# First tokens and weights in slices, ScalarE's table loaded first, normed tokens made before the small vectors

## What is computed

```
h  = rms_norm(x, norm_mix)                 # x * rsqrt(mean(x*x) + eps) * gain
p  = h @ w_in                              # columns: conv x | conv b | conv c | u | gate_a | gate_b
ya = W_conv_out( b * dwconv3_causal(c * x_conv) )
yb = GLU( gelu( Re(C s_t) + D u_t ) ),     s_t = A_bar s_{t-1} + B_bar u_t
x  = x + W_o( sigmoid(gate_a) * ya + sigmoid(gate_b) * yb )
x  = x + HierMoE( rms_norm(x) )            # 32 experts, 512 wide, top 1 group then top 2 experts
out = rms_norm(x)
```

## Time and profile before

| | us |
|---|---|
| median of three executions | 711.07 |
| lowest and highest | 710.84 and 711.48 |
| the profiled execution | 712.18 |
| its span, first to last instruction | 710.5 |
| PE busy in the span | 546.5 (77%) |
| PEld busy | 329.6 (46%) |
| DVE busy | 206.6 (29%) |
| ACT busy | 63.9 (9%) |
| POOL busy | 39.9 (6%) |

### The profile page before, as it was taken

How to read it: one execution, slowest core, us unless ns; L and a number is a source line. 1 busy time by engine, 2 the same in 40 slices (tenths; PEclk the granted TensorE clock), 3 DMA queues, 4 the chain that set the end, 5 groups by cost and what they waited for, 6 DMA issues and landing times.

```text
span 710.5 us, 7587 instructions
## 1 busy us (share of the span) xinstructions
PE 546.5 (77%) x3259; PEld 329.6 (46%) x3259; DVE 206.6 (29%) x443; ACT 63.9 (9%) x128; POOL 39.9 (6%) x68
## 2 busy tenths in 40 slices
PE   8999999999999999898583482594567348247765
PEld 7888888788878456363141140141114114012411
DVE  4888896969423043000000010000000001000002
ACT  3010000002011023000010000000000000000002
POOL 5001111111100011000000000000000000000000
PEclk9999999999999999999896797788779679778988
DMA  8960903274089657999999999999999999999993
GB/s 336 424 288 0 355 2 132 105 266 185 24 351 428 261 215 284 409 428 428 431 427 427 429 429 428 426 431 427 428 429 429 428 428 431 427 428 430 426 425 136
DMA packets 18901, 241.92 MB, mean 341 GB/s; under 512 B 2353, under 2 KB 2481, under 8 KB 4402
## 3 DMA queue, kind: packets, MB, share of 16 engines
q1 hardware_dynamic: 18432, 239.83, 81.1%
q10 hardware_dynamic: 434, 1.58, 0.5%
HBM read 240.35 MB, written 1.05 MB: 340 GB/s over the span
## 4 chain that ended last, share of the span: by engine, by line
PE 52%; DMA 43%; issue 1%; DVE 1%; SPq 1%; ACT 1%; DVEq 0%; POOL 0%; PEldq 0%; ACTq 0%
DMA x_region<-in_w_down 38%; PE bank L1138 28%; PE bank L1399 8%; DMA rot_region<-in_last_halves 4%; PE bank L1272 4%; PE bank L1150 2%; PE bank L1440 2%; PE bank L1127 2%; PE bank L1358 1%; PE bank L1461 1%; PE bank L1391 1%; SPq L474 1%; DMA ring<-in_mix 1%; PE bank L1242 1%; PE bank L1252 1%
## 5 line engine op out<-in xcount | busy, mean ns | idle before, releaser
L1391 PE MATMUL bank<-ring,z_region 128*32 128x512 f32 x672 | 113.2, 681 | 69.3 <-DMA ring<-in_w_up 68.8
L1138 PE MATMUL bank<-x_region,ring 128*128 128x256 f32 x640 | 141.0, 381 | 1.7 <-ACT ring L626 1.1
L1138 PEld LDWEIGHTS bank<-x_region,ring 128*128 128x128 f32 x640 | 120.8, 190 | 21.3 <-ACT ring L626 2.8
L1399 PE MATMUL bank<-ring,z_region 128*32 128x512 f32 x192 | 57.0, 760 | 49.9 <-DMA x_region<-in_w_down 49.9
L1391 PEld LDWEIGHTS bank<-ring,z_region 128*32 128x32 f32 x672 | 30.3, 123 | 113.8 <-issue 113.8
L1062 DVE TENSOR_TENSOR z_region<-z_region,bank 128x512 f32<-128x512 f32 x8 | 8.2, 1026 | 203.5 <-PE bank L1391 191.4
L1391 PE MATMUL bank<-rot_region,z_region 128*32 128x512 f32 x112 | 50.9, 609 | 12.1 <-DMA ring<-in_w_gate 10.5
L1399 PE MATMUL bank<-late_region,z_region 128*32 128x512 f32 x96 | 56.9, 760 | 0.0
L1399 PE MATMUL bank<-x_region,z_region 128*32 128x512 f32 x96 | 56.9, 760 | 0.0
L1399 PEld LDWEIGHTS bank<-ring,z_region 128*32 128x32 f32 x192 | 14.8, 136 | 87.3 <-issue 87.3
L1391 PE MATMUL bank<-s_region,z_region 128*32 128x512 f32 x112 | 51.1, 610 | 0.0
(11 more groups left out here) (245 smaller groups left out, 531.5 us busy)
## 6 DMA issues: line engine op xcount, KB each, us to landing
ring<-in_w_up SPq DMA_DIRECT2D x28, 2048.0 KB, 39.1
ring<-in_mix SPq DMA_DIRECT2D x16, 2048.0 KB, 10.6
ring<-in_w_gate SPq DMA_DIRECT2D x14, 2048.0 KB, 45.6
ring<-in_w_down SPq DMA_DIRECT2D x12, 2048.0 KB, 35.4
ring<-in_first SPq DMA_DIRECT2D x8, 2048.0 KB, 13.0
rot_region<-in_w_gate SPq DMA_DIRECT2D x7, 2048.0 KB, 36.2
s_region<-in_w_gate SPq DMA_DIRECT2D x7, 2048.0 KB, 40.7
late_region<-in_w_down SPq DMA_DIRECT2D x6, 2048.0 KB, 43.0
```

The lines of the kernel that those rows point to most:

```text
L1138: ins = MM(dst, w[:, k, n * P:(n + 1) * P], rhs[:, k, :], start=k == 0, stop=k == kn - 1)
L1391: ins = MM(bank[to][quarter(e), :], xT[:, k, quarter(e)], of_expert[e][:, FF * k:FF * k + FF], start=k == 0, stop=k == KD - 1)
L1399: ins = MM(bank[6 + h][quarter(e), :], actT[:, c, quarter(e)], of_expert[e][:, D * c + 512 * h:D * c + 512 * h + 512], start=c == 0, stop= ...
```

## The change

- `x_columns` is laid out as one array of eight slices and comes in five pieces: slice 0, slice 1, slices 2 and 3, slices 4 and 5, slices 6 and 7. Unit 0 comes in eight pieces, one for each slice k, each directly behind the piece of x that it is used with. All of it stays on SP's queue, behind the vectors and ahead of all else.
- ACT copies two constants as its first instruction, behind a small wait for POOL, so that its table load comes ahead of the wait for the vectors and x.
- DVE makes `hT` directly behind `zc`, ahead of the twenty operations on 16 columns.
- PE waits for each slice of unit 0; the sum of squares moves from behind k = 2 to behind k = 3, and the row of 1/rms from behind k = 4 to behind k = 5.

```
-            for c in range(U_PIECES):
-                sp.dma_start(x_raw[:, 2 * c:2 * c + 2, :].rearrange("p k t -> p (k t)"), x_columns[c]).then_inc(x_cols_in[c], 16)
-                if c == 0:
-                    first_piece(0)
-            for c in range(1, U_PIECES):
-                first_piece(c)
+            for (k0, k1), landed in zip(X_PIECES, x_cols_in):
+                sp.dma_start(x_raw[:, k0:k1, :].rearrange("p k t -> p (k t)"), x_columns[:, T * k0:T * k1]).then_inc(landed, 16)
+                for k in range(k0, k1):
+                    sp.dma_start(w8(U_U)[:, k, :], mix[U_U, :, 512 * k:512 * k + 512]).then_inc(u_in[k], 16)
...
-            nc.gpsimd.memset(halfneg[:], -0.5)
+            nc.gpsimd.memset(halfneg[:], -0.5).then_inc(halves_set, 1)
...
+            act.wait_ge(halves_set, 1)
+            nc.scalar.activation(stat[:, 0:2], halfneg[:], ACT.Copy)
+
             act.wait_ge(cols_in, 16)
             for k in range(KD):
-                if k % 2 == 0:
-                    act.wait_ge(x_cols_in[k // 2], 16)
+                for (k0, _), landed in zip(X_PIECES, x_cols_in):
+                    if k == k0:
+                        act.wait_ge(landed, 16)
...
-            for piece in range(U_PIECES):
-                dve.wait_ge(x_cols_in[piece], 16)
+            for piece in range(PAIRS):
+                if piece == 0:
+                    dve.wait_ge(x_cols_in[0], 16)
+                dve.wait_ge(x_cols_in[piece + 1], 16)
...
             ins.then_inc(zc_ready, 1)
+
+            dve.wait_ge(row_ready, 1)
+            dve.wait_ge(h_raw_ready, KD)
+            for piece in range(PAIRS):
+                V.tensor_tensor(hT[:, 2 * piece:2 * piece + 2, :], h_raw[:, 2 * piece:2 * piece + 2, :],
+                                rstd_row.unsqueeze(1).to_broadcast([P, 2, T]), ALU.mult).then_inc(hT_ready, 2)
...
-            dve.wait_ge(row_ready, 1)
-            dve.wait_ge(h_raw_ready, KD)
-            for piece in range(U_PIECES):
-                V.tensor_tensor(hT[:, 2 * piece:2 * piece + 2, :], h_raw[:, 2 * piece:2 * piece + 2, :],
-                                rstd_row.unsqueeze(1).to_broadcast([P, 2, T]), ALU.mult).then_inc(hT_ready, 2)
...
             for k in range(KD):
-                if k % 2 == 0:
-                    pe.wait_ge(u_in[k // 2], 16)
+                pe.wait_ge(u_in[k], 16)
                 pe.wait_ge(h_raw_ready, k + 1)
...
-                if k == 2:
-                    pe.wait_ge(square_step, 2 * U_PIECES - 1)
+                if k == 3:
+                    pe.wait_ge(square_step, 2 * PAIRS - 1)
...
-                if k == 4:
+                if k == 5:
                     pe.wait_ge(diag_ready, 1)
```

More of the change, by code:

```diff
@@ L31 @@
 MIX_UNITS = 17
-U_PIECES = 4
+X_PIECES = ((0, 1), (1, 2), (2, 4), (4, 6), (6, 8))
+PAIRS = KD // 2
 U_BANKS = (2, 3, 6, 7)
@@ L170, in block_kernel @@
         gate_b = ring[:, MIX_RING, 0:KD * T].rearrange("p (k t) -> p k t", k=KD)
-        squares = ring[:, MIX_RING, 0:KD * T].rearrange("p (c n) -> p c n", c=U_PIECES)
+        squares = ring[:, MIX_RING, 0:KD * T].rearrange("p (c n) -> p c n", c=PAIRS)
         square_sum = ring[:, MIX_RING, KD * T:KD * T + 2 * T]
@@ L241, in block_kernel @@
         consts = sem("consts")
+        halves_set = sem("halves_set")
         pool_step = sem("pool_step")
@@ L247, in block_kernel @@
         rstd = sem("rstd")
-        x_cols_in = [sem(f"x_cols_in{i}") for i in range(U_PIECES)]
-        u_in = [sem(f"u_in{i}") for i in range(U_PIECES)]
+        x_cols_in = [sem(f"x_cols_in{i}") for i in range(len(X_PIECES))]
+        u_in = [sem(f"u_in{i}") for i in range(KD)]
         h_raw_ready = sem("h_raw_ready")
@@ L421, in _ @@
             sp.dma_start(cols[:], columns[:]).then_inc(cols_in, 16)
-            def first_piece(c):
-                sp.dma_start(w8(U_U)[:, 2 * c:2 * c + 2, :].rearrange("p k n -> p (k n)"),
-                             mix[U_U, :, 1024 * c:1024 * c + 1024]).then_inc(u_in[c], 16)
-            for c in range(U_PIECES):
-                sp.dma_start(x_raw[:, 2 * c:2 * c + 2, :].rearrange("p k t -> p (k t)"), x_columns[c]).then_inc(x_cols_in[c], 16)
-                if c == 0:
-                    first_piece(0)
-            for c in range(1, U_PIECES):
-                first_piece(c)
+            for (k0, k1), landed in zip(X_PIECES, x_cols_in):
+                sp.dma_start(x_raw[:, k0:k1, :].rearrange("p k t -> p (k t)"), x_columns[:, T * k0:T * k1]).then_inc(landed, 16)
+                for k in range(k0, k1):
+                    sp.dma_start(w8(U_U)[:, k, :], mix[U_U, :, 512 * k:512 * k + 512]).then_inc(u_in[k], 16)
             for u in range(1, MIX_UNITS):
@@ L1574, in laid_out @@
     halves = last[KF - 1].reshape(P, PACK, 2, 512).transpose(2, 0, 1, 3)
-    x_columns = one["x"].reshape(T, U_PIECES, 2, P).transpose(1, 3, 2, 0).reshape(U_PIECES, P, 2 * T)
+    x_columns = one["x"].reshape(T, KD, P).transpose(2, 1, 0).reshape(P, KD * T)
     return {"x": inputs["x"], "x_columns": x_columns, "columns": columns, "mix": mix, "s5_b": s5_b.reshape(P, -1), "s5_c": s5_c.reshape(P, -1),
```

## The result

The changed kernel takes 714.64 us (median of 18 executions, 711.97 to 716.73) against 711.49 for the kernel before (18, 710.57 to 713.6). The ratio is 1.0041, 95% interval 1.0032 to 1.0049: some 2.9 us slower. Forecast were 710.2, a range of 708.5 to 711.8, and a chance of 0.08 for slower.

What follows compares the result with a forecast made beforehand. The prediction took PE's opening, held at c by unit 3's landing, to bound the kernel. Of a possible 2.7 us, 1.8 becomes a wait at c, leaving 0.9: 711.07 − 0.9 = 710.2 us, range 708.5 to 711.8.

Steps and rivals of the forecast that it cites:

- What bounds the kernel: Whole kernel: PE's lead before the experts moves the end by as much; c waits for unit 3, slack 1.0 us.
- Start: First matmul of line 1150: starts at 5.1 us instead of 6.47, and the idle 1.31 us vanishes.
- clock: TensorE in the opening: with no gap it reaches full clock by about 6.6 us, not 10.0; line 1150 ends 2.7 sooner.
- Landings by bytes in today's rows: Early transfers: landings follow bytes at 354 KB per us, putting x's last piece near 11.2 us.
- at 29.8 as today: Unit 3, which c needs: its landing is unchanged at 29.8 us, between 27.5 and 31.1.
- the gain of 0.9: Start of c: PE waits for unit 3 until 29.8 + 0.05 instead of starting at 30.78, gaining 0.9 us.
- the 1.3 us that the prediction left to chance: Unit 3 landed 6.2 us behind unit 2, against 4.9 by bytes; which unit pays the 1.3 us is chance.
- No wait, by 0.2: Sum of squares: ready at 12.65 us, PE reaches it behind k = 3 at 12.9, so no wait.
- up to 0.5: Squares and 1/rms: a later x shifts both by up to 0.5 us, hidden by what follows.
- Rival 4: Wait at c: TensorE's clock falls in 1.8 us idle, price 1.8 us; time 711.9, a loss of 0.9; chance 0.06.
- Rival 3: Early queue: small pieces slow it, c's unit lands late; at 31.1 the kernel loses 0.3, 711.4; chance 0.10.
- Parts costed at nothing: Table load hidden today, up to 0.4 us in the new order; earlier hT earns nothing alone; zb, first convolution hidden.

Runs made afterwards that it cites:

- e5: Changed kernel with the sum of squares moved behind k = 5 and the row of 1/rms behind k = 7; 1.0037 of the kernel before.
- e6: Kernel before with the early table load and hT ahead of the small operations, transfers as before; ratio 1.0003.
- e3: Kernel before with unit 0's four pieces as blocks in DRAM, 4 KB rows side by side; ratio 0.9977.
- e10: Kernel before with unit 0 as eight blocks of 2 KB rows in DRAM, sent as eight transfers; ratio 1.0010.
- e8: Kernel before with unit 0's four pieces as blocks, plus the early table load and earlier hT (e3 and e6 together); ratio 0.9990.
- e11: e8 with the two state matrices sent behind unit 3 and zb, zc made ahead of the first convolution; 1.0001 of the kernel before.
- e9: Kernel before with unit 0 as eight blocks of 2 KB rows in DRAM, still four transfers; ratio 1.0001.
- e1: Changed kernel, same pieces and order, with each piece of x and unit 0 one block in DRAM; 1.0002 of the kernel before.
- e13: Changed kernel with only unit 0's slices as blocks in DRAM, x's pieces still rows 8 KB apart; 1.0018 of the kernel before.
- e14: Kernel before with x's pieces as 2 KB rows 8 KB apart, its own four pieces, order and unit 0 kept; ratio 1.0011.
- e2: Changed kernel with only x's pieces as blocks in DRAM, unit 0 still 2 KB rows 16 KB apart; one run, no ratio given.

## Why the prediction was wrong, by its own steps

**What bounds the kernel: right.** The mixer handed on the opening's loss whole in every trace, and in ten of the twenty c waits for unit 3. In the other ten, the changed kernel's first among them, PE came to c later than unit 3.

**Start right, clock right by luck.** First row at 4.95 (5.1 forecast). Unit 0's first slice landed at 4.5 to 4.9 (4.6 forecast). The 16 rows of k = 0 and 1 took 3.73 to 3.91 in the changed kernel's three traces, the clock up about at once; the forecast had 6.6 us, and gave the missing gap as the reason. The runs don't bear that reason out. In e5's two traces, with the same start and no gap, the 16 rows took 5.01 and 5.04. With a gap of 1.24 us (e6), 0.98 (e3) and 1.95 (e10) the first 24 rows took 5.42 to 5.45, the clock up at once, and with gaps of 0.23 (e8) and 0.70 (e11) they took 6.59 and 8.10. What decides the rise stays open.

**"Landings by bytes in today's rows": this is the step that failed.** It made every landing from bytes at 354 KB per us (its own two landings give (3126 − 822) / (12.4 − 6.42) = 385, and x's last piece at 11.1; the slip changes nothing here), and bounded the price of the new pieces by 0 to 0.9 us. x's last piece was put at 11.2 and landed at 14.4, 13.8 and 14.2. Unit 3 was taken "at 29.8 as today" and landed at 31.8, 31.1 and 32.1, so that by this term alone the gain of 0.9 became a loss of 0.3 to 1.4. The rows taken as nearest were x's pieces of 2 KB rows, but those lay side by side in one block, and the new ones don't.

The landings say what stood in its place: four more transfers in unit 0, 0.9 us, all of it on the first two slices (e9, e10); rows 16 and 8 KB apart, 1.7 (17.0 to 15.3, e1; from the nearest and the farthest of six traces with and two without, 0.9 to 2.4), with the time coming down by 0.39%. The other 0.9, from e10's 14.4 to e1's 15.3, came with x in five pieces and the new order, which no run takes apart. Unit 3 was less late (2.0, 1.3 and 2.3) than the last matrix (3.2, 2.7 and 3.1), because in the kernel before it landed 6.2 us behind unit 2 and in the changed kernel 4.9, 4.9 and 5.5: the 1.3 us that the prediction left to chance did not fall on unit 3 in two traces of three, and that made the loss smaller.

**"No wait, by 0.2": failed with it.** A margin of 0.2 us was treated as cover, and lateness "up to 0.5" as the most. It was 3.2, and PE idled 2.74 and 1.09 at the squares in two traces, 1.82 and 2.05 at k = 2 in the second and third.

**Rival 4: the mechanism was right, the place was not.** It put the fall of the clock in a wait at c and priced it 1.8 us. It happened at the squares, or at k = 2, and cost (1.87 + 5.94) − (0.79 + 3.56) = 3.5 us at the first trace's squares. **Rival 3** was the one that came true: the queue was slowed and unit 3 was late, though more by how the pieces lie than by their being small. But its bound for slower by over 0.2% (a landing at 32.2, at c alone) left out that the same lateness also stops PE inside u. The mean opening is 2.2 us longer, which the floor and this together give; the chance for slower, 0.08 in all, was too small.

**Parts costed at nothing: right.** Table load and `hT` (e6: 1.0003). `zb` and the first convolution stayed off PE's path in the changed kernel.

The Trainium skill's "DMA: Bandwidth & Descriptors", section "Rules for kernel authors", advises putting many small transfers together. It had the sign right, and the prediction set it aside, because the page's figures were far off here: pieces of 256 KB land 0.65 us apart once the queue runs, in all these kernels. What it speaks of, the number of transfers, is the part of 0.9 us, paid once and not for each transfer. That same-sized pieces side by side in DRAM are faster than rows far apart is shown by e1, e13 and e14.

What stays open: why one hole comes behind the first 822 KB and why rows 8 or 16 KB apart make it longer, when behind it the same kind of slices land 0.65 us apart; what sets the clock's rise; and the last 1 us between traces and medians (e5, e9).

## What to carry to other kernels

When pieces are cut smaller, look at how each lies in DRAM: a slice of a wider array is not the block that it replaces, and a layout in which each piece is one block was worth 0.3 to 0.4% here for the same pieces, and 0.23% to the kernel before (0.10% and nothing in e8 and e9, its near twins). A transfer that stands behind all others in a full queue (unit 3) pays for the delays ahead of it, so starting its consumer sooner gains only down to its landing. And a cover of 0.2 us is none: price the wait behind it, with the clock's fall.

## What was not expected of the hardware

- Early transfers with both kinds of rows far apart moved 156 to 229 GB/s between 5 and 9 us over six traces, with the engines' share at 0.65 to 0.92; the same pieces as blocks 258 and 285; the kernel before 331 and 345.
- The length of PE's idle time alone did not decide whether the clock fell: behind 1.11 us (e1) and 1.28 (e13) it fell, behind 1.14 (e2), and 1.82 and 1.09 (the changed kernel, second trace) it did not, behind 2.05, 2.46 and 2.74 it did.
- The rise differs between executions of like kernels: the first 24 rows of u took 5.42 and 5.45 in e3 and e6, 7.43 and 7.20 in the kernel before, 8.10 in e11.
- Behind the first nine or ten issues on SP one or two took 0.86 to 1.47 us in place of 0.43 in the six traces (unit 0's sixth slice 1.24 in the changed kernel), so unit 1 was issued at 9.6 to 10.3, not 8.7. By the landings that cost nothing: unit 1 was in 4.9 us behind the last matrix, as in the kernel before.
- From 4 to 7 us no kernel here moved more than 365 GB/s (e9) and most moved 202 to 302, against 428 to 432 later.
